# Unit matmuls walk their 256 columns in another order: groups of four, from both halves of the row in turn, last group first

## What is computed

```python
# first block
h = rmsnorm(x, norm_mix);  p = h @ w_in            # 2048 -> 4352
y = concat(pool_mixer(p), hyena_mixer(p), chunked_gating(p))
x = x + y @ w_out                                  # 2048 -> 2048
h = rmsnorm(x, norm_ffn);  up = dwconv3(h @ ffn_w_up)   # 2048 -> 11264
gate, val = split(up)
x = x + (silu(gate) * val) @ ffn_w_down            # 5632 -> 2048
x = rmsnorm(x, norm_final)
# second block
proj = rms_norm(x) @ w_in_2                        # 2048 -> many heads and gates
ya = band_attention(...); yb = rwkv7_time_mix(...); yc = memory_cross_attention(...)
merged = sigmoid(ga)*(ya @ w_up_a) + sigmoid(gb)*(yb @ w_up_b) + sigmoid(gc)*(yc @ w_up_c)
return x + merged @ w_o
```

## Time and profile before

| | |
|---|---|
| median of 3 runs | 2315.16 us (2314.85 to 2325.08) |
| the profiled execution: span of its instructions | 2314.3 us |
| TensorE matmuls | 22,128, busy 2298.7 us |
| unit matmuls among them (256 columns, float32r) | 17,616 |
| VectorE busy | 1529.2 us |
| ScalarE busy | 1114.5 us |
| memory traffic | 173 GB/s mean |
| granted TensorE clock | 1.000 throughout |

### The profile page before, as it was taken

How to read it: one execution, slowest core, us unless ns; L and a number is a source line. 1 busy time by engine, 2 the same in 40 slices (tenths; PEclk the granted TensorE clock), 3 DMA queues, 4 the chain that set the end, 5 groups by cost and what they waited for, 6 DMA issues and landing times.

```text
span 2314.3 us, 54222 instructions
## 1 busy us (share of the span) xinstructions
PE 2298.7 (99%) x22128; PEld 2264.9 (98%) x22128; DVE 1529.2 (66%) x2109; ACT 1114.5 (48%) x1513; POOL 12.8 (1%) x27
## 2 busy tenths in 40 slices
PE   8999999999999999999999999999999999999999
PEld 7999999999999999999999999999999999999999
DVE  7668767666545666678786677777767555555554
ACT  6443445555434555444644455555546444444442
POOL 0000000000000000000000000000000000000000
PEclk9999999999999999999999999999999999999999
DMA  7553556555555555655554444343434455556554
GB/s 272 168 178 120 181 181 195 187 190 186 187 190 186 188 190 186 223 186 179 195 177 147 132 141 132 129 148 126 135 125 139 163 186 189 190 185 189 190 186 162
DMA packets 110533, 401.44 MB, mean 173 GB/s; under 512 B 12538, under 2 KB 12565, under 8 KB 110240
## 3 DMA queue, kind: packets, MB, share of 16 engines
q1 hardware_dynamic: 108288, 390.91, 51.6%
q0 software_dynamic: 2080, 8.06, 1.1%
HBM read 396.81 MB, written 2.10 MB: 172 GB/s over the span
## 4 chain that ended last, share of the span: by engine, by line
PE 97%; DVE 2%; DMA 0%; issue 0%; ACT 0%; SPq 0%; DVEq 0%; ACTq 0%
PE bank L473 96%; DVE w_lo L1650 1%; DMA raw<-in_units 0%; DVE x L1699 0%; ACT w_hi L1102 0%; PE bank L908 0%; DVE prod L1696 0%; DVE acc L1696 0%; DVE scaled_in L1696 0%; PE bank L834 0%; ACT x L1185 0%; SPq L1067 0%; SPq L1072 0%; DVE fh L1703 0%; PE bank L1009 0%
## 5 line engine op out<-in xcount | busy, mean ns | idle before, releaser
L1650 DVE TENSOR_TENSOR w_lo<-raw,w_hi 128x1024 fp32r<-128x1024 f32 x736 | 894.6, 1223 | 637.4 <-ACT w_hi L1102 632.3
L1102 ACT ACTIVATE w_hi<-raw 128x1024 fp32r<-128x1024 f32 x736 | 778.6, 1059 | 855.2 <-PE bank L473 846.3
L473 PE MATMUL bank<-h_hi,w_hi 128*128 128x256 f32 x4016 | 1134.7, 283 | 8.9 <-DVE h_lo L1699 8.9
L473 PE MATMUL bank<-h_lo,w_hi 128*128 128x256 f32 x4016 | 1121.9, 279 | 0.0
L473 PE MATMUL bank<-h_hi,w_lo 128*128 128x256 f32 x4016 | 1121.2, 279 | 0.0
L473 PEld LDWEIGHTS bank<-h_hi,w_hi 128*128 128x128 f32 x4016 | 755.5, 188 | 15.0 <-DVE h_lo L1699 8.9
L473 PEld LDWEIGHTS bank<-h_lo,w_hi 128*128 128x128 f32 x4016 | 755.7, 188 | 1.6
L473 PEld LDWEIGHTS bank<-h_hi,w_lo 128*128 128x128 f32 x4016 | 755.4, 188 | 0.0
L473 PE MATMUL bank<-m_hi,w_hi 128*128 128x256 f32 x704 | 196.7, 279 | 0.0
L473 PE MATMUL bank<-m_lo,w_hi 128*128 128x256 f32 x704 | 196.5, 279 | 0.0
L473 PE MATMUL bank<-m_hi,w_lo 128*128 128x256 f32 x704 | 196.5, 279 | 0.0
(11 more groups left out here) (434 smaller groups left out, 2734.8 us busy)
## 6 DMA issues: line engine op xcount, KB each, us to landing
raw<-in_units SPq DMA_DIRECT2D x736, 512.0 KB, 3.6
memx<-in_memT POOLq DMA_DIRECT2D x4, 512.0 KB, 8.1
out_y<-obuf SPq DMA_DIRECT2D x8, 256.0 KB, 4.4
x<-in_xT SPq DMA_DIRECT2D x3, 512.0 KB, 9.0
bias_t<-in_bias POOLq DMA_DIRECT2D x8, 192.0 KB, 2.6
dft<-in_dft POOLq DMA_DIRECT2D x1, 1024.0 KB, 10.9
decay<-in_decay POOLq DMA_DIRECT2D x1, 768.0 KB, 7.7
x<-in_xT SPq DMA_DIRECT2D x2, 256.0 KB, 4.5
```

Of the source, the lines that this page charges most:

```text
L473: return pe.matmul(out, lhsT, rhs, start=start, stop=stop, skip_group_check=True)
L1102: return act.activation(out, in_, ACT.Copy, scale=scale)
L1650: dve.tensor_tensor(w_lo[slot][:, :, :], raw[slot][:, :, :], w_hi[slot][:, :, :].bitcast(F32), ALU.subtract).then_inc(split_done, 1)
```

## The change

A helper `turned` gives another view of a row of 256 elements: the row is cut into two halves (`q`) of 32 groups (`s`) of four elements (`e`), and walked with the group index outermost and descending, the half next, the four elements innermost and ascending. So the order is elements 124 to 127, 252 to 255, 120 to 123, 248 to 251, and so on down to 0 to 3 and 128 to 131. Each unit matmul uses this view for the activations that it reads and for the PSUM columns that it writes, so that every result lands at the place where it was. Weights, weight loads, semaphores, loops, and all other matmuls are as before.

```diff
 UN = 256
+LINE = 4
...
+        def turned(ap2d):
+
+            return ap2d.rearrange("p (q s e) -> p s q e", q=2, e=LINE)[:, ::-1, :, :]
+
...
                     for t in range(tiles):
                         wh = w_hi[slot][:, kk, t * P:(t + 1) * P]
                         wl = w_lo[slot][:, kk, t * P:(t + 1) * P]
-                        rh, rl = hi[:, k0 + kk, :], lo[:, k0 + kk, :]
-                        mm(o[:, t, :], wh, rh, first and kk == 0 and t == 0, False)
-                        mm(o[:, t, :], wh, rl, False, False)
-                        m = mm(o[:, t, :], wl, rh, False, last and kk == UK - 1 and t == tiles - 1)
+                        out = turned(o[:, t, :])
+                        rh, rl = turned(hi[:, k0 + kk, :]), turned(lo[:, k0 + kk, :])
+                        mm(out, wh, rh, first and kk == 0 and t == 0, False)
+                        mm(out, wh, rl, False, False)
+                        m = mm(out, wl, rh, False, last and kk == UK - 1 and t == tiles - 1)
...
-                                o = p2(pair[t // 2])[:, t % 2, :]
+                                o = turned(p2(pair[t // 2])[:, t % 2, :])
                                 wh, wl = wh4[:, kk, t * P:(t + 1) * P], wl4[:, kk, t * P:(t + 1) * P]
-                                rh, rl = m_hi[:, 2 * u + kk, :], m_lo[:, 2 * u + kk, :]
+                                rh, rl = turned(m_hi[:, 2 * u + kk, :]), turned(m_lo[:, 2 * u + kk, :])
```

More of the change, by code:

```diff
@@ L754, in part @@
                         wl = w_lo[slot][:, kk, t * P:(t + 1) * P]
[L755 to L758, removed]
+                        out = turned(o[:, t, :])
+                        rh, rl = turned(hi[:, (k % 4) * UK + kk, :]), turned(lo[:, (k % 4) * UK + kk, :])
+                        mm(out, wh, rh, k % 4 == 0 and kk == 0 and t == 0, False)
+                        mm(out, wh, rl, False, False)
+                        m = mm(out, wl, rh, False, k % 4 == 3 and kk == 3 and t == 1)
                 if half != 0:
```

## The result

The changed kernel takes 2466.99 us (median of 4 runs, 2465.94 to 2467.57), the kernel before 2316.03 us in the same comparison: 1.0636 times the time, 95% interval 1.0614 to 1.0658. It is slower by 6.4%, where 2185 us was forecast. The profiled execution has a span of 2464.9 us, 150.6 more than before.

The account below looks back on a forecast made before the run. TensorE's pitch of 116.7 ns over 17,616 unit matmuls was taken as the bound. Span 2314.3 - 132 (pitch 109.2) + 2 (start waits) = 2184, plus 0.9 to the median: 2185 us; 8-in-10 range 2138 to 2338.

Parts of the forecast that it names:

- What bounds the kernel: TensorE, 99% busy: the 116.7 ns pitch of 17,616 unit matmuls makes 2055 us of the span.
- The loss grows with the columns; it lies in the stream, not in issue, and not in the weight load: Unit matmuls: 10 ns of each pitch, 176 us in all, attributed to streaming the columns.
- The same to 0.1 ns over every tile, in every stage: Unit matmuls: the 10 ns loss taken as uniform, so either a path ceiling or a straight walk's self-collision.
- Order can be a term of a pitch: Transposes on TensorE: 120 ns with a stepped weight operand against 109, read as order affecting pitch.
- I take the collision, and that the new walk is free of it: Unit matmuls: straight walk collides with itself, turned walk doesn't; pitch 109.2 ns, 132 us less; faster 0.44.
- Groups of four break up no pair: Activation reading: jumps fall only between whole 16-byte groups, unlike the stepped load's 0.52 ns a jump.
- each jump costs: Rival, unit matmuls: 63 jumps add 5.5 or 33 ns of pitch, 2412 or 2896 us; chance 0.23.
- The ceiling: Rival, unit matmuls: the path gives 2.19 values a nanosecond in any order, so no change, 2315 us; chance 0.33.
- The accumulation and the other engines: PSUM accumulation unhurt, other engines' work untouched; VectorE and ScalarE idle time down about 130 us each if right.
- The rule on writing: PSUM writes: non-contiguous access slows matmuls significantly; by it 2412 us or far above, on the slower rival's side.
- Its rule on reading: SBUF activation reads: strides free with at least two hits a 16-byte line, so groups of four cost nothing.

Follow-up runs that it names:

- e8: Kernel before, but every unit matmul reads the row's first four positions 64 times, plain writing; 2233.95 us, pitch 111.7 ns.
- e10: Kernel before, but each unit matmul's weight load reads one element 128 times; 2282.35 us, pitch 113.3 ns in one stage, 116.7 in another.
- e1: Changed kernel with only the activation reading turned, PSUM written in plain order; 2467.98 us, pitch 125.3 ns.
- e3: Changed kernel without the alternating halves: groups of four, last group first, in reading and writing; 2333.05 us, pitch 117.8 ns.
- e4: Changed kernel walked upwards: groups of four from the two halves in turn, first group first, reading and writing; 2489.96 us, pitch 126.7 ns.
- e2: Changed kernel with only the PSUM writing turned, activations read in plain order; 2317.63 us, pitch 116.7 ns.
- e17: Kernel before, but groups of four walked ascending in steps of 64 bytes, reading and writing; 2282.86 us beside 2316.56, pitch 114.8 ns in the last stage.
- e7: Kernel before, but groups of four walked ascending in steps of 256 bytes, reading and writing; 2605.93 us, pitch 133.3 ns.
- e9: Kernel before, but the two halves read and written in turn, ascending, in groups of 16 columns (15 jumps); 2371.79 us, pitch 120.0 ns.
- e14: Changed kernel with unit matmul operands taken as plain float32, at half the column rate; 7862.06 us, pitch 215.8 ns.
- e18: Kernel before with plain reading, but PSUM written in groups of two columns from the two halves in turn; 2322.66 us.
- e13: Kernel before, but halves read and written in turn, ascending, in groups of two columns (127 jumps); 3232.68 us, pitch 164.4 to 173.3 ns.

## Why the prediction was wrong

- **What bounds the kernel** was right: the span moved by the pitch of 17,616 matmuls and by nothing else.
- **"The loss grows with the columns; it lies in the stream, not in issue, and not in the weight load"** stands for the columns, and not wholly for the load. e8 splits the loss: 5.0 of the 10 ns go when the row is not walked, and 5.0 are left even then. But e10, which changes only the place that the weight load reads, takes 3.3 of the 10 ns away in the feed-forward block. One load for 512 columns as for 256 was no proof that it has no part.
- **"The same to 0.1 ns over every tile, in every stage"** was read from two stretches and is not so. In the kernel before, 56 us of the first projection hold 478 matmuls and 56 us of the down projection 482 (both counts with the few under way at the window's start). From start to start that is 117.8 and 116.7 ns.

```profile
80.00:136.00 56.00, 56.00 (x478) 56.00 (x477) 34.68 (x45) 26.16 (x30) 0.00 (x0) 1.00 0.58 182
640.00:696.00 56.00, 56.00 (x482) 56.00 (x481) 26.88 (x25) 21.24 (x20) 0.00 (x0) 1.00 0.59 189
```

- **"Order can be a term of a pitch"** was right, and in both directions (114.8 to 173 ns in kernels that compute the same result).
- **The step that failed** is "I take the collision, and that the new walk is free of it", with its term of 132 us less. Measured, that term is 153 us more. Nothing in the rows said that alternating 512 bytes apart is a good order; it was preferred as the most different one. What the runs show in its place: reading from the two halves in turn adds 8.7 ns (10.0 going up; e1, e3, e4), and the turned writing adds nothing (e2). e17 shows that a better order than the plain one exists, by 1.9 ns, and e4 and e7 that the walks with the large distances are bad ones.
- **"Groups of four break up no pair"**, and so cost nothing to read, was wrong too: whole groups of 16 bytes are not enough, at any of the far distances.
- **The rival "each jump costs"** has the right sign. Its two prices, 5.5 and 33 ns a matmul (2412 and 2896 us), lie on both sides of the measured 8.7 ns. But it was priced by the number of jumps, and e3 and e4 show the same number at 1.1 and 10.0 ns: where the jumps go matters more than how many there are, though at one distance their number counts too (e9). By the rows its chance of 0.23 looks too low. The transposes and the strided load of the earlier trace rows, the only rows where order differs, show losses from leaving the plain order, large and small, and no gain; they spoke for this rival.
- **The ceiling** at 116.7 ns is none: e17 reads the same values in 114.8 ns and e8 as many in 111.7. What may be left of it are the 5.0 ns that stay in e8, and the freedom at half rate in e14 fits it.
- **The accumulation and the other engines** behaved as described; their idle time grew.
- **The rule on writing** of the Trainium skill (PSUM — Partial Sum Buffer, Specifications) is not borne out here: a write that is not contiguous costs 0 in groups of four (e2), and between 1.1 ns less and 1.1 ns more in groups of two (e18). Its rule on reading (SBUF — State Buffer, in Door 1: The DMA port swizzle), full bandwidth with at least two hits on a 16-byte line, fails as well: two hits a visit take 164 to 173 ns (e13), four take 126.7 with the halves in turn (e4). The same note of the Trainium skill adds that each access that crosses to a new line pays a penalty. With twice the crossings e13 fits that in sign. But in groups of four all orders cross as often as the plain walk does, and take 114.8 to 133.3 ns.

Open is the mechanism. It looks as if certain places of a row got in each other's way when they are read in turn, which is argued and not shown. It could as well hang on the turns back, which no run parts from the distance. The runs don't say either why 64 bytes are better than 16, nor why the place of the weight load matters in some stages and not in others.

## What to carry to other kernels

Where TensorE runs back to back in float32r, the order in which the moving operand is read is part of the price, and the order of writing hardly was, in the two orders tried: keep the layout that reads in place, and put a permutation that is needed on the output side. A loss whose cause isn't known is no evidence that any other order lacks it; weigh the rows in which order already differs, and try a small series of distances on one matmul before changing them all. In plain float32, at half the column rate, the turned order was free.

## What was not expected of the hardware

- Plain walks of float32r lose 10 ns over 106.7 in 256 columns; 5.0 of them remain even when the same 16 bytes are read 64 times (e8).
- The pitch does not rise steadily with the distance of groups: 116.7, 117.8, 114.8, 123.6, 133.3 ns at 16, 32, 64, 128 and 256 bytes.
- Descending is cheaper than ascending when the halves alternate (125.3 against 126.7 ns), dearer by 1.1 ns when they don't.
- Turned writing to PSUM in groups of four costs nothing measurable (500.80 us in the last piece in both kernels), and in groups of two 1.1 ns at most, in either direction.
